# Inner norms of a two-block transformer kernel: right halves of the rows behind the first operand chunks, products of high parts first

## What is computed

```python
def first_block(x, ...):
    h = rms_norm(x, pre_mix_norm)
    ...                                           # mixers
    x = x + rms_norm(mixed @ w_out, post_mix_norm)
    h = rms_norm(x, pre_ffn_norm)                 # norm 0
    u = causal_dwconv(h @ ffn_w_up, ...)
    ...
    x = x + rms_norm(f, post_ffn_norm)
    return x                                      # norm 1, with the second block's first norm

def second_block(x, ...):
    h = rmsnorm(x, ln_attn_pre)
    mix = token_mixer(h, w_in, ...)
    x = x + rmsnorm(mix @ w_out, ln_attn_post)
    h = rmsnorm(x, ln_mlp_pre)                    # norm 2
    u = jnp.square(jax.nn.relu(h @ w_up))
    return x + rmsnorm(u @ w_down, ln_mlp_post)   # norm 3, the output
```

## Time and profile before

| | before |
|---|---|
| median of three runs | 944.78 us |
| the profiled execution | 944.75 us, span 943.0 us |
| PE busy | 880.5 us, 93% |
| DVE busy | 598.0 us, 63% |
| ACT busy | 480.5 us, 51% |
| POOL busy | 136.1 us, 14% |
| mean granted TensorE clock | 0.976 |

### The profile page before, as it was taken

One profiled execution on the slowest core, in us unless ns is written; L12 is line 12 of the kernel. 1 busy time (PEld: TensorE's weight loads), 2 busy tenths in 40 slices (PEclk: granted clock), 3 DMA queues, 4 the chain that ended last, 5 costly groups with the idle time before them and its releaser, 6 DMA issues.

```text
span 943.0 us, 15727 instructions
## 1 busy us (share of the span) xinstructions
PE 880.5 (93%) x6246; PEld 813.5 (86%) x6246; DVE 598.0 (63%) x721; ACT 480.5 (51%) x692; POOL 136.1 (14%) x122
## 2 busy tenths in 40 slices
PE   3999888999999999898999999799998999999997
PEld 3999787999988998788899998688886799999995
DVE  4448756535777578666777777666545576655654
ACT  5356763236755534366666656464435344343332
POOL 0025661100000032023333233000000000000000
PEclk9999898999999999999999999799999999999999
DMA  8442333232432445544545465233321536555541
GB/s 328 158 179 91 134 134 134 88 122 105 146 138 108 157 149 191 196 170 145 185 174 187 178 221 181 90 134 134 135 90 68 178 113 223 179 178 183 193 157 45
DMA packets 21735, 143.82 MB, mean 153 GB/s; under 512 B 3008, under 2 KB 3012, under 8 KB 5168
## 3 DMA queue, kind: packets, MB, share of 16 engines
q1 hardware_dynamic: 19872, 138.30, 41.0%
q0 software_dynamic: 1808, 4.73, 1.4%
HBM read 141.96 MB, written 1.84 MB: 152 GB/s over the span
## 4 chain that ended last, share of the span: by engine, by line
PE 63%; DVE 14%; ACT 10%; issue 7%; POOL 4%; DMA 1%; ACTq 0%; SPq 0%; DVEq 0%; POOLq 0%
PE pj L480 12%; PE pj L483 9%; PE pj L482 9%; ACT w_hi L1113 4%; PE pa L875 4%; PE pa L876 4%; PE pa L877 4%; DVE w_lo L1561 4%; DVE area L1574 4%; POOL area L439 3%; DVE area L1577 3%; PE pj L484 2%; PE pj L485 2%; PE pa L519 2%; ACT area L1395 1%
## 5 line engine op out<-in xcount | busy, mean ns | idle before, releaser
L1561 DVE TENSOR_TENSOR w_lo<-w_raw,w_hi 128x2048 fp32r<-128x2048 f32 x128 | 303.4, 2373 | 92.1 <-ACT w_hi L1113 92.1
L480 PE MATMUL pj<-a_hi,w_hi 128*128 128x256 f32 x1184 | 341.4, 288 | 14.1 <-DVE w_lo L1561 10.0
L482 PE MATMUL pj<-a_lo,w_hi 128*128 128x256 f32 x1184 | 337.7, 285 | 0.0
L483 PE MATMUL pj<-a_hi,w_lo 128*128 128x256 f32 x1184 | 337.6, 285 | 0.0
L1113 ACT ACTIVATE w_hi<-w_raw 128x2048 fp32r<-128x2048 f32 x128 | 242.9, 1905 | 71.7 <-PE pa L877 38.6
L480 PEld LDWEIGHTS pj<-a_hi,w_hi 128*128 128x128 f32 x1184 | 230.2, 194 | 20.4 <-issue 17.8
L482 PEld LDWEIGHTS pj<-a_lo,w_hi 128*128 128x128 f32 x1184 | 230.1, 194 | 0.8
L483 PEld LDWEIGHTS pj<-a_hi,w_lo 128*128 128x128 f32 x1184 | 229.8, 194 | 0.0
L875 PE MATMUL pa<-w_hi,a_hi 128*128 128x512 f32 x280 | 110.1, 393 | 4.1 <-issue 2.5
L876 PE MATMUL pa<-w_lo,a_hi 128*128 128x512 f32 x280 | 109.9, 393 | 0.0
L877 PE MATMUL pa<-w_hi,a_lo 128*128 128x512 f32 x280 | 109.6, 391 | 0.0
(11 more groups left out here) (249 smaller groups left out, 1119.2 us busy)
## 6 DMA issues: line engine op xcount, KB each, us to landing
w_raw<-stream SPq DMA_DIRECT2D x128, 1024.0 KB, 4.8
area<-gains POOLq DMA_DIRECT2D x4, 512.0 KB, 4.1
cst<-consts SPq DMA_DIRECT2D x1, 1093.0 KB, 13.4
x_tok<-x_in SPq DMA_DIRECT2D x2, 512.0 KB, 4.4
area<-cmpw POOLq DMA_DIRECT2D x1, 1024.0 KB, 5.4
out<-x_tok SPq DMA_DIRECT2D x4, 256.0 KB, 2.0
t_wide<-t_rows POOLq DMA_DIRECT2D x1, 768.0 KB, 13.1
prm<-params SPq DMA_DIRECT2D x1, 562.5 KB, 10.0
```

Source lines behind the costliest of these rows:

```text
L480: pe.matmul(out_, a[0], a[1], start=first, stop=False)
L482: pe.matmul(out_, wh, al, start=False, stop=False)
L483: return pe.matmul(out_, wl, ah, start=False, stop=last)
L1561: dve.tensor_tensor(w_lo[:, slot, :], w_raw[:, slot, :], w_hi[:, slot, :].bitcast(F32), ALU.subtract)\
```

## The change

In the inner norms, DVE's order becomes: left halves of both row blocks, split of chunks 0 and 1, rows 0 right, low part of chunk 2, rows 1 right, low parts of chunks 3 to 7. Chunks 2 and 3 are turned into bank 2 and chunks 4 and 5 into bank 1 (`turned`), since bank 1 (rows 0 right) is now read later. PE turns the first rows' chunks 0 and 1, does the warm-up, then turns the rest of chunks 0 to 3. Chunks 4 to 7 are turned ahead of chunk 3 instead of chunk 2. In each chunk PE does the eight products with `a_hi` first and the four with `a_lo` behind them; for chunks 0 and 1 the first eight wait for the high part only (`x_hi`), and the gate on the low part stands between. The last norm keeps its order (`y_final`).

```diff
+        def turned(j, k):
+            q = k // 2
+            return pa[:, (0, 2, 1, 3)[q] if j else q, (k % 2) * T:(k % 2 + 1) * T]
...
                 turn_x(j, 0, 0, 1)
+                keep_warm(2, WARM)
+                turn_x(j, 0, 1, 2)
                 turn_x(j, 1, 0, 2)
-                keep_warm(2, WARM)
-                turn_x(j, 0, 1, 3)
-                turn_x(j, 1, 1, 4)
+                turn_x(j, 1, 1, 3)
...
                 for k in range(KC):
-                    if k == 2:
-                        for q in (2, 3):
-                            turn_x(j, q, 0, 5)
-                            turn_x(j, q, 1, 5)
-                    gate(k)
+                    if k == 3:
+                        turn_x(j, 2, 0, 4)
+                        turn_x(j, 2, 1, 5)
+                        turn_x(j, 3, 0, 5)
+                        turn_x(j, 3, 1, 5)
+                    if k < 2:
+                        pe.wait_ge(S("x_hi"), 2 * j + k + 1)
+                    else:
+                        gate(k)
                     for i in range(2):
-                        slot = (u + i) % SLOTS
                         for nb in range(2):
-                            mm = three_acc(pj[b[i][0]][:, nb * T:(nb + 1) * T], slot, k * 256 + nb * P, k,
-                                           k == 0 and nb == 0, k == KC - 1)
+                            first_hi(pj[b[i][0]][:, nb * T:(nb + 1) * T], (u + i) % SLOTS, k * 256 + nb * P, k, nb == 0)
+                    if k < 2:
+                        gate(k)
+                    for i in range(2):
+                        for nb in range(2):
+                            mm = first_lo(pj[b[i][0]][:, nb * T:(nb + 1) * T], (u + i) % SLOTS, k * 256 + nb * P, k)
...
+            def first_hi(o_, slot, c, k, fresh):
+                pe.matmul(o_, w_hi[:, slot, c:c + P], a_hi[:, k, :], start=(k == 0 and fresh), stop=False,
+                          skip_group_check=True)
+                pe.matmul(o_, w_lo[:, slot, c:c + P], a_hi[:, k, :], start=False, stop=False, skip_group_check=True)
+
+            def first_lo(o_, slot, c, k):
+                return pe.matmul(o_, w_hi[:, slot, c:c + P], a_lo[:, k, :], start=False, stop=(k == KC - 1),
                                  skip_group_check=True)
...
+            def y_norm(j, gname):
+                dve.wait_ge(S("gbc_loaded"), 16 * (j + 1))
+                y_bias(j, 0)
+                y_recip(j, 0)
+                x_add(0, 0, 512, "x_ready")
+                y_bias(j, 1)
+                y_recip(j, 1)
+                x_add(1, 0, 256, "x_ready")
+                x_add(1, 256, 512, "x_ready")
+                g = prm_(gname)
+                dve.wait_ge(S("x_turned"), 4 * j + 1)
+                for k in range(2):
+                    dve.tensor_scalar(a_hi[:, k, :], turned(j + 1, k), g[:, k:k + 1], None, ALU.mult)\
+                       .then_inc(S("x_hi"), 1)
+                    dve.wait_ge(S("x_hi"), 2 * j + k + 1)
+                    stt(a_lo[:, k, :], turned(j + 1, k), g[:, k:k + 1], a_hi[:, k, :].bitcast(F32), ALU.mult,
+                        ALU.subtract).then_inc(S("opnd_lo"), 1)
+                y_gain(j, 0, 1)
+                x_add(0, 512, 1024, "x_ready")
+                operand_lo(j + 1, gname, 2)
+                y_gain(j, 1, 1)
+                x_add(1, 512, 1024, "x_ready")
+                for k in range(3, KC):
+                    operand_lo(j + 1, gname, k)
```

More of the change, by code:

```diff
@@ L541, in turn_x @@
                 for k in (2 * q, 2 * q + 1):
-                    o = (k % 2) * T + tb * P
-                    mm = transpose(pa[:, q, o:o + P], x_tok[:, tb, k * P:(k + 1) * P])
+                    mm = transpose(turned(j + 1, k)[:, tb * P:(tb + 1) * P], x_tok[:, tb, k * P:(k + 1) * P])
                 if tb == 1:
@@ L1142, in operand @@
                         await_psum(act, "ST"[k // 4], "x")
-                    act.activation(a_hi[:, k, :], pa[:, k // 2, (k % 2) * T:(k % 2 + 1) * T], ACT.Copy,
-                                   scale=g[:, k:k + 1]).then_inc(S("opnd_hi"), 1)
+                    act.activation(a_hi[:, k, :], turned(j, k), ACT.Copy, scale=g[:, k:k + 1]).then_inc(S("opnd_hi"), 1)
             def x_squares(j, junk_):
@@ L1595, in operand_lo @@
                 dve.wait_ge(S("opnd_hi"), (k | 1) + 1 + (6 * j if j else 0))
-                stt(a_lo[:, k, :], pa[:, k // 2, (k % 2) * T:(k % 2 + 1) * T], g[:, k:k + 1],
-                    a_hi[:, k, :].bitcast(F32), ALU.mult, ALU.subtract).then_inc(S("opnd_lo"), 1)
+                stt(a_lo[:, k, :], turned(j, k), g[:, k:k + 1], a_hi[:, k, :].bitcast(F32), ALU.mult, ALU.subtract)\
+                    .then_inc(S("opnd_lo"), 1)
             def x_spread(j, before_rbc=None):
@@ L1620, in x_add, with y_bias, y_recip @@
                     .then_inc(S(done), 1)
-            def y_norm(j, gname=None):
+            def y_bias(j, tb):
+                dve.wait_ge(S("y_sq"), 4 * j + 2 * tb + 1)
+                dve.tensor_scalar(ybias[:, tb:tb + 1], ysum[:, 2 * tb:2 * tb + 1], 1.0 / D, EPS, ALU.mult, ALU.add)\
+                   .then_inc(S("y_bias"), 1)
+                y_gain(j, tb, 0)
+            def y_recip(j, tb):
+                dve.wait_ge(S("rms_root"), 2 * j + tb + 1)
+                V_.did(dve.reciprocal(yr[:, tb:tb + 1], yrt[:, tb:tb + 1]))
+                V_.sync()
@@ L1625, in y_norm, with y_final @@
+            def y_final(j):
                 dve.wait_ge(S("gbc_loaded"), 16 * (j + 1))
                 for tb in range(2):
[L1627 to L1651, removed]
@@ L1652, in y_norm @@
-                    y_gain(j, tb, 1)
[L1653 to L1656, removed]
+                    y_bias(j, tb)
+                    y_recip(j, tb)
+                    x_add(tb, 0, 512, "x_final")
+                    y_gain(j, tb, 1)
+                    x_add(tb, 512, 1024, "x_final")
+            def y_norm(j, gname):
[22 more added lines that the diff above has]
+                    operand_lo(j + 1, gname, k)
@@ L2193, in _ @@
             ffn2_step(UP2 - 1, UP2 // 3, 0)
-            y_norm(3)
+            y_final(3)
 def pack(v):
```

## The result

| | before | after |
|---|---|---|
| median of nine runs taken together | 944.48 us (939.15 to 945.13) | 935.04 us (934.28 to 938.94) |
| ratio | | 0.993, 95% interval 0.9909 to 0.9952 |
| the profiled execution | 944.75 us, span 943.0 | 938.94 us, span 937.1 |
| first bias of norm 0 to the next unit | 20.68 us | 19.14 us |
| first bias of norm 1 to the copy of the scale | 22.91 us | 19.31 us |

Executions of one and the same kernel differ here by up to 6 us, with the times at which TensorE is at the lower clock, so medians of few runs mislead; the ratio is the number to go by. It says 6.6 us (0.7% of 944.78), between 4.5 and 8.6; forecast were 4.6.

A forecast was written before the change was run, and what follows sets the result against it. TensorE sets the pace, so gains lie where it stands still: 1.37 + 1.40 + 0.85 = 3.62 us from the norms plus 1.0 of clock, 4.6, giving 940.2 us, range 937.6 to 943.2.

The forecast's parts named there:

- Part 1: Inner norms: VectorE's right-half work moves back, so the second rows' bias starts 1.39 us earlier and the root just hides.
- Part 2: First product waits for the high part instead of the low: starts 1.89 us earlier, 0.5 of it from this.
- Part 3: Norm 0: new 0.27 us gap before chunk 2, chunks 4 to 7 turned at 400.34, pair ends 1.6 us earlier.
- Part 4: Behind the pair, the next unit's low half limits; gains 1.37 us in norm 0, 1.40 norm 1, 0.85 norm 2.
- The clock in norm 1: Work filling two idle places brings TensorE's full clock back sooner; 1.0 us taken, bounds nothing to 3.05.
- The sum: Whole kernel: 3.62 us from the three norms and 1.0 of clock, 4.6 in all.
- (e): The forecast itself: gains in the three norms plus 1.0 us of clock, 940.2 us; chance 0.39.
- (b): Rival: the clock in norm 1 gives all of its 3.05 us, 938.2 us; chance 0.15.
- (c): Rival: two more lower-clock stretches between norm 1 and norm 2 hand the gain back, 943.6 us; chance 0.17.
- The sign that the prediction names: Profile after: the prediction is wrong if the lower-clock stretches after norm 1 change in number.
- (d): Rival: VectorE's order delays the last sum of x and TensorE's turns, +2.6 us, 947.4; chance 0.07.
- Loads of weights saved or added: Weight-reuse rule would add 32 loads per pair; the profile row shows none was saved before, so the sum stays.

The follow-up runs named there:

- experiment 1: Changed kernel with the old product order in each chunk, so all products of a chunk wait for its low part again; 935.31 us, ratio 0.9943.
- Experiment 4: Changed kernel with the next unit's split moved forward on ScalarE and VectorE; 935.51 us, ratio 0.9932.
- experiment 2: Kernel before with only high-part products first and chunks 0 and 1 waiting for the high part; 936.71 us, ratio 0.9948.
- filled: Kernel before with twelve more warm-up passes on TensorE ahead of norm 1's first turn; norm 1 19.39 us, whole kernel 938.16 us, ratio 0.9972.

## Why the prediction was right or wrong

**Part 1, right halves back:** right. The first bias to the second shrank by 1.38 (1.39 forecast), the root hid, and the warm-up was what came last: turn of the second rows at 392.44, 3.35 behind the first bias; forecast 394.60 - 391.24 = 3.36.

**Part 2, high parts first:** right at its place, 4.40 from first bias to first product (forecast 4.42, before 6.31). Its use is small: experiment 1 puts it at 0.26 a norm, the gap ahead of chunk 2 takes the other half, and in norm 0 the next stage takes back most of what is left. The prediction had the gap; it had missed that the new order makes the first unit end later, and that ACT's split and DVE's low half hang on that. This is the step that the working left out: 0.26 us in the next stage, 0.16 of it seen at that wait.

**Part 3, what is late next:** the gap and the turns at 9.05 behind the first bias (forecast 9.10) are right, and so is the end of the pair, 17.12 (forecast 17.2).

**Part 4, the end of the pair:** the mechanism is right, and the copy does stand behind the low half of the next unit. Norm 0 gave 1.54 (forecast 1.37), norm 1 at full clock 1.39 (forecast 1.40), norm 2 0.95 (forecast 0.85). Sum 3.88 against 3.62. The 0.17 of norm 0 comes from the turns (0.20 earlier instead of 0.15) and from the copy, which starts 0.08 ahead of the recorded end of the low half and not 0.03 behind it. Experiment 4 shows norm 2's limit. That norm 1 hits its forecast so well is in part luck: the 1.40 was worked out with the lower clock up to the third chunk, the 1.39 was measured without it.

**The clock in norm 1:** the term with the widest bounds, 0 to 3.05, taken as 1.0. In the first profiles it was 2.2 (3.60 - 1.39). Two profiles of each kernel give 22.91 and 21.00 before, 19.31 and 20.23 after; their means differ by 2.2, of which 0.8 is clock. The prediction also misread where the clock falls: not in the 3.25 us without work, but with the first turn behind them (granted clock 1.00 from 594.0 to 597.5, 0.50 from there to 607.7). After, it was low from 593.3 to 596.7, so the warm-up at 594.49 started 1.2 us behind the fall and not 2. The reason given, that the new order closes the gaps in which the clock stays low, is not shown: experiment 2 had the gap ahead of the warm-up and a short stretch all the same, and so had the kernel before in its second profile (596.3 to 599.7). What is shown is that the clock costs up to 3.5 in norm 1 (22.91 against 19.39 filled).

**The sum.** 4.6 forecast, 6.6 measured (4.5 to 8.6). The three norms and the next stage give 3.9 - 0.26 + 0.1 = 3.7. The rest, 2.9 us with an interval from 0.8 to 4.9, is in no stretch that repeats; all that the profiles show for it is the clock of norm 1 and of the stages around it, where single executions differ by more. How much of it the change brings about stays open. Part of it may be the draw: the forecast counted from 944.78, the median of three long executions, while 29, 21 and 11 executions of the kernel before, timed beside the experiments, have medians of 941.02, 940.61 and 940.67. So the forecast's range holds the difference but not the time itself, 935.04 against 937.6 to 943.2. Among executions with nearly the same mean granted clock the kernels differ by about 5 us: 939.0 to 939.6 before at 0.985 (three of the 29), 934.3 to 934.6 after at 0.984; 940.0 to 940.7 at 0.978 (eight), 934.9 at 0.977. The forecast's likeliest case (e) names the right parts. The first profile lies between (e) and (b): the products of chunks 0 and 1 were back at full clock, the warm-up was not (2.40 to the next turn, before 2.56): 2.2 of the 3.05. That 6.6 us less than 944.78 is just the 938.2 of (b) is chance.

**Rivals.** (c), handed back in later low stretches: the first profile has it, 2.30 us of it, and the other profiles show that it belongs to neither kernel. The sign that the prediction names, another number of low stretches behind norm 1, tells nothing: in the attention stage both profiles before have three, and of the changed kernel the first has three (two of them longer) and the second one. (d), DVE's order as bound: no; the last sum of x ended at 397.94 and PE reached the turns at 398.14, 0.20 to spare (0.24 forecast). Loads of weights saved or added by the order of the products do not come in: norm 0 has 125 of them from bias to release both before and after, as the row of loads had said.

## What to carry to other kernels

Cut a step's time into the stretch from its first instruction to what it releases, and compare that: where the clock was full it repeated to 0.02 us, while whole executions differed by 6. When a queue's order is changed to start earlier, look at what signals completion too: products of both units side by side start sooner, but end the first unit late, and whatever takes over its slot pays (0.16 to 0.26 us here). And after a wait is shortened, the engine that was ahead of it is often next: here the split of a unit that could have been made in another engine's idle time, which gave norm 2 another 0.67.

## What was not expected of the hardware

The same instructions up to norm 0 took from 387.2 to 391.5 us in these profiles, and the attention stage from 127.7 to 133.1; the difference that the traces show is the granted clock (1.2 or 2.4 GHz), low at other places and for longer or shorter. This kernel, with waits on TensorE in many spots, so has a set of times and not one. Twelve passes whose result nobody reads, put into a single gap, took some 2.6 us off the kernel before.
